# Stick-breaking attention: the third projection block of a head moves to the seam before that head

## What is computed

```python
z = einsum('bqhd,bkhd->bhqk', qb, k) * scale
log_1mb = where(strict, log_sigmoid(-z), 0)
between = cumsum(log_1mb, reverse=True) - log_1mb
w = where(strict, exp(log_sigmoid(z) + between), 0)
out = einsum('bhqk,bkhd->bqhd', w, v)
```

## Time and profile before

| | us |
|---|---|
| median of 3 runs | 2133.34 (2132.6 to 2137.78) |
| the profiled execution, its own time | 2134.68 |
| its span in the trace | 2132.9 |
| TensorE busy, matmul | 1897.1 (89%) |
| VectorE busy | 1346.2 (63%) |
| ScalarE busy | 1085.5 (51%) |
| GpSimd busy | 549.9 (26%) |
| mean granted TensorE clock | 0.929 |

### The profile page before, as it was taken

The page is one execution under the profiler, slowest core; times in us unless marked ns, Lnnn a source line. Parts: engine busy times, 40 slices in busy tenths (PEclk is TensorE's granted clock), DMA queues, the critical chain, the costliest instruction groups (busy, mean ns, idle before and its releaser), DMA issues.

```text
span 2132.9 us, 34211 instructions
## 1 busy us (share of the span) xinstructions
PE 1897.1 (89%) x11552; PEld 1600.2 (75%) x11552; DVE 1346.2 (63%) x2807; ACT 1085.5 (51%) x2406; POOL 549.9 (26%) x436
## 2 busy tenths in 40 slices
PE   6999997899999999999998689888488888888998
PEld 6999997777777777777787577766366666667886
DVE  7606885676767676766766613334578888874544
ACT  6422111665666566666656523333377878872221
POOL 0000000343434444444444300011134444440000
PEclk9999998898989898999999779999689999999999
DMA  6322131001010000101000112133801313014542
GB/s 219 96 69 64 65 117 49 6 6 25 5 25 12 18 18 13 24 6 25 5 25 6 45 50 78 53 116 107 190 3 37 74 28 82 8 64 174 183 153 79
DMA packets 121866, 129.28 MB, mean 61 GB/s; under 512 B 81936, under 2 KB 94992, under 8 KB 120464
## 3 DMA queue, kind: packets, MB, share of 16 engines
q1 hardware_dynamic: 121744, 127.86, 20.6%
HBM read 85.89 MB, written 41.94 MB: 60 GB/s over the span
## 4 chain that ended last, share of the span: by engine, by line
PE 67%; DVE 15%; ACT 7%; issue 7%; DMA 2%; POOL 1%; SPq 0%; DVEq 0%; ACTq 0%; POOLq 0%
PE ps L647 6%; PE ps L601 6%; PE ps L603 5%; PE ps L602 5%; PE ps L588 4%; PE ps L589 4%; PE ps L590 4%; PE ps L633 4%; DVE small L1480 3%; PE ps L826 3%; PE ps L875 3%; PE ps L877 3%; PE ps L876 3%; PE ps L621 3%; PE ps L784 2%
## 5 line engine op out<-in xcount | busy, mean ns | idle before, releaser
L1623 POOL TENSOR_TENSOR ring_r<-ring,sp_hi 128x512 fp32r<-128x512 f32 (+1 forms) x320 | 358.5, 1120 | 838.0 <-DVE sp_hi L1343 838.0
L647 PEld LDWEIGHTS ps<-v,ring 128*128 128x128 f32 x2176 | 303.8, 202 | 37.2 <-issue 13.3
L647 PE MATMUL ps<-v,ring 128*128 128x65 f32 x2176 | 299.9, 280 | 5.0 <-ACT ring L1000 3.3
L988 ACT ACTIVATE ring<-ps 128x512 f32<-128x512 f32 (+1 forms) x320 | 170.5, 533 | 256.2 <-PE ps L622 194.9
L1642 POOL TENSOR_TENSOR p<-p 128x1024 f32<-128x1024 f32 (+4 forms) x96 | 170.5, 1788 | 246.5 <-ACT p L1135 246.5
L601 PE MATMUL ps<-ht_hi,w_hl 128*128 128x512 f32 x448 | 201.1, 449 | 30.1 <-DVE ring L1437 9.7
L588 PE MATMUL ps<-w_hl,ht_hi 128*128 128x256 f32 x768 | 212.9, 277 | 0.7 <-DVE w_hl L1221 0.6
L589 PE MATMUL ps<-w_hl,ht_hi 128*128 128x256 f32 x768 | 212.6, 277 | 0.0
L590 PE MATMUL ps<-w_hl,ht_lo 128*128 128x256 f32 x768 | 212.6, 277 | 0.0
L1340 DVE SCALAR_TENSOR_TENSOR ring<-ring,ps 128x512 f32<-128x512 f32 (+1 forms) x320 | 192.0, 600 | 30.0 <-ACT ring L993 29.2
L1126 ACT ACTIVATE p<-ps,small 128x1024 f32<-128x1024 f32 (+4 forms) x192 | 164.4, 862 | 69.2 <-DVE small L1484 63.2
(11 more groups left out here) (183 smaller groups left out, 3992.4 us busy)
## 6 DMA issues: line engine op xcount, KB each, us to landing
w_raw<-in_w_narrow SPq DMA_DIRECT2D x18, 512.0 KB, 4.1
xb<-in_x SPq DMA_DIRECT2D x16, 512.0 KB, 3.9
gate_scr<-ring SPq DMA_DIRECT2D x64, 128.0 KB, 1.8
w_raw<-rot_scr SPq DMA_DIRECT2D x32, 256.0 KB, 3.6
qk_scr<-w_hl SPq DMA_DIRECT2D x32, 256.0 KB, 3.3
gb<-gate_scr SPq DMA_DIRECT2D x16, 512.0 KB, 3.6
yb<-y_scr SPq DMA_DIRECT2D x16, 512.0 KB, 4.5
xr<-in_x SPq DMA_DIRECT2D x16, 512.0 KB, 4.2
```

The source lines that it names most:

```text
L647: mm = pe.matmul(ps[:, 4 + i % 2, j * (HD + 1):(j + 1) * (HD + 1)], ring[:, 4 + i % 2, j * P:(j + 1) * P], v1[:, kb, :], start=True, stop= ...
L1623: nc.gpsimd.tensor_tensor(ring_r[:, i % 4, j0 * P:], ring[:, i % 4, j0 * P:], sp_hi[:, i % 4, j0 * P:].bitcast(F32), ALU.subtract).then_in ...
```

## The change

Block 2 is no longer projected in slots 5 to 8 of its own head, but in slots 39 to 42 of the head before. Blocks 0 and 1 of the next head move from slots 28 to 31 and 36 to 39 to slots 25 to 28 and 32 to 35. Block 3 stays at slots 14 to 17. The split of the weights starts at slot 18 and not 20. For head 0 block 2 is projected in slots 0 to 3 of the lead, behind a wait for the stack of block 1. Since at + 6 would be slot 45 for the block at 39, VectorE does both of its operations in slot 44. The amount of work is the same.

```diff
-SB_PROJECT = ((0, 2, 5), (0, 3, 14), (1, 0, 28), (1, 1, 36))
-SB_SPLIT = 20
+SB_PROJECT = ((0, 3, 14), (1, 0, 25), (1, 1, 32), (1, 2, 39))
+SB_SPLIT = 18
...
             for i in range(SB_LEAD):
+                if i == 0:
+                    pe.wait_ge(sp_act, 6)
+                    pe.wait_ge(sp_dve, 4)
+                if i < 4:
+                    project(C_SB, 2, 7, sp_ps, i)
                 sb_slot(0, i, True)
...
+            for k in range(3):
+                sb_stack_hi(0, 2, k)
...
                         sb_stack_lo(h, ahead * NT + n, i - at - 5)
+                    if i == at + 5 == SB_LEAD + N_ST - 1 and more:
+                        sb_stack_lo(h, ahead * NT + n, 1)
...
+            for k in range(2):
+                sb_stack_lo(0, 2, k)
```

## The result

The changed kernel takes 2223.0 us in the median of four runs (2210.4 to 2244.7), the kernel before 2135.6 in four runs beside it: a ratio of 1.0385 [1.0329, 1.0441]. The ratio is the recorded one of the fast executions, without the longest; the quotient of the two medians is 1.041. I had forecast 2178 and a range up to 2202. The direction was right, the size was half of what came, and the time lies outside the range.

A forecast was written before the change was run, and what follows sets the result against it. TensorE was taken to set the pace, with time lost to waits and the half clock behind them. Terms without the clock gave -29 us, new clock falls +74, together +45 on 2134.68: median 2178, range 2108 to 2202.

The forecast's parts named there:

- Slot 12, -53: Slot 12: the stack wait of 2.46 us in eight heads goes (19.7), with 33.6 of clock loss behind it.
- The seam, -34, and the small waits, -15: Slots 39 to 44: waits of 11.3 and clock loss of 22.9 go; small waits elsewhere go, 7 x 2.1 us.
- Two stack waits, +42: Slots 32 and 39: projections seven slots apart wait 3.0 us each for the stack, 7 x 6.0 us.
- The clock behind them, +48: Behind slots 32 and 39: clock at 0.50 for at least 6.8 us, losing 3.4 each, 14 times.
- Slots 43 to 8, +28: Slots 43 to 8 without projection: 1.95 us wait before slot 7's sums plus smaller waits, 3.5 a head, eight heads.
- Behind slot 7 I take the loss per seam, 22.9 / 7 = 3.3: Behind slot 7's wait: the clock falls and loses 3.3 us in each of eight heads, 26 in all; bound 5.1 each.
- Weights two slots earlier: Slots 18 to 20: the earlier split meets block 3's stack, adding 0.4 us a head of waits, +3 in all.
- rival D: Slots 20 to 23: waits of 0.99 and 0.83 grow, the clock falls, 8 x 3.4 = 27 us more: 2205; chance 0.10.
- The lead, 0: Before head 0: later start and projection in slots 0 to 3 cost +5, offset by -5.6 from slots 5 to 8.
- A: Chiefly slots 32 and 39: the new waits come but the clock holds, -29 us: 2104, faster; chance 0.15.
- B: Slots 32 and 39: the two stack waits are short, 0.6 us, without their clock loss: 2096; chance 0.06.
- C: Clock falls at only some of slots 32, 39 and 7: 2154, 2152 or 2130 depending on which; chance 0.27.

The follow-up runs named there:

- the kernel with both mends: Changed kernel with blocks 0 and 1 projected at slots 23 and 31, split from 16, VectorE's loop turn behind slot 23: 2135.9 us, 0.9995 of the kernel before.
- the kernel with block 3 put back at slot 14: Version with projections at slots 10, 24, 32, 41, split from 16, VectorE's turn behind 25 (2079.1 us), but block 3 at 14: 2123.9 us, 0.9946.

## Why the prediction was wrong

**Slot 12, -53: half right.** The wait went, as said. The clock behind it did not come back, because the stretch that starts at slot 6 or 7 covers slot 12 in six heads out of eight; it ends there in slots 12 to 14.

**The seam, -34, and the small waits, -15: right.** In the trace of before the waits in slots 42 to 44 are 14.5 us in all (the row of slot 44 that I took, 0.24, is the smallest; five heads have 0.86 to 0.88), those in slots 27 and 36 10.0; after the change all of them are gone, and the falls at slots 43 and 44 with them.

**Two stack waits, +42: right.** 38.6 us, from two rows about a slot four later. The measured 2.76 each lies between my bounds.

**The clock behind them, +48: right in place, too high.** It fell at slots 32 and 39 in all seven heads. The loss was 35.0.

**Slots 43 to 8, +28: near in size, wrong in cause in six heads of eight.** I had computed a wait of 1.95 before the sums of step 44 in slot 7. In heads 0 and 7 it is there with 1.46 and 1.45. In the others TensorE waits one slot earlier and before other matmuls, 3.4 to 3.6 each; all waits of slots 5 to 7 together are 33.1 us. The cause is the turn of VectorE's loop, which in the trace of before stands as 17.2 us of "issue" in six times, 2.9 each. I had read the waits of TensorE and had left out those of an engine that was not late. The cover for them was exactly the projection that the change moves.

**The step that failed: "Behind slot 7 I take the loss per seam, 22.9 / 7 = 3.3".** The term was 8 x 3.3 = 26 and measured 65.3, that is 8.2 a head, outside my bound of 5.1. The seven stretches of the seam lasted mostly 6.8 us, and behind each of them dense projection slots came at once. I took their length for a property of a fall. In heads 2 and 6 of the changed kernel it was 6.8 too, but in the others 17.1 to 27.3, with TensorE busy for 25.97 of 27.30 us. Two runs show the cause: projections six slots earlier, or matmuls that do nothing, cut the stretches to 6.8, with one of 10.2 in each. Why two heads came off with 6.8 without either is open.

**The second step that failed: "Weights two slots earlier", +3 and nothing for the clock.** It was rival D in place and size: I had that with 8 x 3.4 = 27 us and a chance of 0.10; the fall came in all eight heads with 38.5, and the range left it out. Its mechanism is not borne out: I had the waits of 0.99 and 0.83 grow, and 1.01 and 0.27 stand there. What made the clock fall behind waits that are no longer than before is not shown. I trusted the gap of 0.99 with the clock unmoved. But 0.99 had held in one place and 0.90 had not in another; that should have given this rival more than a tenth, and it was the only one that adds to the forecast instead of taking its place.

**The lead, 0: right in its parts.** The scores of step 0 started 8.1 us later, but those of slot 5 only 4.6 (387.62 against 383.01), where I had +5. The 5.6 of the parts left slots 5 to 8, where the half clock hides what they gave.

**The sum.** Without the clock the executions differ by 102 - 82.4 = 19.6 us in these stages (102 is 915.4 - 821.7 + 8.1, rounded). My terms other than the clock's come to -29 + 56.5 = 27.5 when the 56.4 of old falls, 33.6 and 22.9, are put with the clock. So these terms were right together within 8 us and the clock's were not: 138.8 us lost after, where I had 74. Of the rivals, A is refuted (the falls came at all places), B too (2.76 and not 0.6), C describes no head, E fell. The clock's miss of 65 is 39 behind slot 7 and 38.5 at slot 22, less 13 at the stack waits.

The Trainium skill ("TensorE: Matmul & The Clock Gate", "Loop structure matters more than you think") shows a copy on VectorE as leaving the matmuls warm, where the next matmuls follow at once. Here TensorE has to wait for VectorE, and the trace has a stretch at 0.50 at each of the fourteen waits of 2.76 us.

## What to carry to other kernels

Price a possible fall of the clock by the work that follows it, not by the length of other falls: count the time to the next dense block of matmuls, and put that block close behind every place that may wait. When a block of dense work is moved, list what it covered on every engine, the loop's turn and other "issue" gaps included, since these show in the waits of engines that are not late. A one-constant edit that touches a place with a wait near one that lost the clock elsewhere is worth its own line in the range.

## What the runs showed of the hardware

**A long stretch at 0.50 in a busy engine.** From 744.8 to 772.1 TensorE was busy 95% of the time at the half clock and did not get the full one back; in the kernel with both mends it was busy for 13.70 of 13.70 us at 0.50 in slots 8 to 12. At the place of the first the full clock was back after 10.2 us with 15 more matmuls in five slots. Slots of scores, sums and values alone brought it back too, but later: in five of the six long stretches of the changed kernel it returned in slots 12 and 13, 0.9 to 2.3 us before the first matmul of the projection. What decides when it comes back is not settled here.

**The turn of a loop.** On VectorE it costs 2.4 to 2.7 us at slot 44 in the changed kernel, 2.8 to 2.9 before and 3.6 to 4.8 with two stack operations fewer in front of it. The matmuls of TensorE and the work of ScalarE go through the same turn without idle time of more than 0.1 us that the trace puts down to issue. At slot 15 or 23 no gap of that kind is left in VectorE's waits; behind slot 25 there is one of 2.6 to 2.9 in six heads that nobody waits for. The Trainium skill ("Runtime: NRT & Kernel Launch", "Instruction fetch mechanics") says that a taken branch to a page that is not at hand stalls until that page is fetched. That fits a gap without a releaser of some us that follows the place of the branch; why it is long at some places and short at others no run here shows.

**Waits and the clock.** In the heads of all traces a wait of TensorE of 2.4 us or more stood at or just ahead of a stretch at 0.50, but for one: 2.86 us in front of slot 32 in head 4 of the kernel with the split at slot 20, with the clock at 1.00 from 931 to 947.

```profile
937.87 0.50 PE L601 MATMUL ps<-ht_hi,w_hl 128*128 128x512 f32 x1 [2.86 <-DVE sb_s L1377]
```

Shorter waits did both, and their length does not tell which. At slots 22 and 23 the waits of 0.99 and 0.83 cost nothing in any head of the kernel before; with the split two slots earlier 1.01, 0.27 and 0.33 cost the clock in all eight. In the kernel with block 3 put back at slot 14 all heads wait 0.76 to 0.78 us in slot 8; in four of them the clock falls in slots 8 or 9, and in four it does not.
